# Twenty unread TensorE turns at the start of a one-core hybrid decoder layer, taken out

## The chip, the cores and the metric

One core of one Trainium2 chip runs the whole layer in one launch. The metric is the device time of that launch in microseconds (us); lower is better. The kernel before was timed three times: 916.11, 916.15 and 916.73 us, median 916.15 us.

## What is computed

The input is a residual stream `x` of 512 tokens by 1024 features and a conditioning row `c` of 1024 values. Cut to what matters here, the reference does:

```
mod = silu(c) @ w_ada + b_ada                       # 1024 x 6144 weights
sh1, sc1, gt1, sh2, sc2, gt2 = split(mod, 6)
h = rms_norm(x, g_norm_mix) * (1 + sc1) + sh1       # 512 x 1024
proj = h @ w_in                                     # columns split into branches
...                                                 # recurrence, attention, merge, x += ...
h2 = rms_norm(x, g_norm_ffn) * (1 + sc2) + sh2
x = x + (1 + gt2) * ((gelu(conv(u_gate)) * u_val) @ w_down)
return rms_norm(x, g_final)
```

The change lies in the first 20 us, where `h` is made: `x` has to be loaded, normalised by token and turned (TensorE works on features by tokens), and the first two parts of `mod` (`sh1` and `sc1`) have to be summed from `w_ada` before the turned `x` can be scaled.

## The kernel before, in words

The kernel has a hand-written instruction stream for each engine: TensorE (PE), VectorE (DVE), ScalarE (ACT), GpSimd (POOL), and SyncE (SP), which issues almost all DMAs. They meet at semaphores. PSUM's eight banks are handed out by a plan made ahead (`plan_banks`); `claim(engine, name)` waits until the bank planned for that name is free, `filled` and `ready` mark and await its contents.

Products are made in three passes over fp32r halves: high weights by high activations, low weights by high activations, high weights by low activations (`three_passes`, `grown`, L1311 is the matmul helper). Work is cut into units of 256 weight columns. Each unit's weights are loaded by SP, rounded to a high part by ACT (`w_hi`) and subtracted to a low part by POOL (`w_lo`, L813, or L824 at the start).

The first three units are "grown": they don't wait for all of `h`. The 1024 features are cut in four shares `j` of 256; as soon as share `j` of `h` exists, TensorE adds its part to the units (`growing_products(j)`).

The order at the start, engine by engine:

- SP loads `c`, the four token tiles of `x`, then for each share `j` the `w_ada` quarters (`ada_quarters(j)`, L628) and the three weight shares (`first_shares(j)`, L637). From `j = 2` on `ada_quarters` waits for the summed pair `j - 2` (`pair_done`), and at `j = 2` also for the bank `("mod1", 0)` to be filled by TensorE.
- ACT squares and sums the four tiles of `x` (L974), POOL takes the inverse root (L760, L761), ACT and DVE write the normalised `x`, two tiles each (`xn_in`, L977 and L1876).
- DVE sums `csilu * w_ada` feature tile by feature tile (`pair_sums`, L1833 to L1837) and, once TensorE has summed over the partitions, finishes `a1` and `mod` (`modulated`, L1849 to L1853).
- ACT then writes `h_hi` and `h_tmp` from the turned `x` (`first_h`, L944); POOL or DVE makes `h_lo` (L794, L1859).
- TensorE turns `c` (`"cT"`), waits for seven small vectors loaded by ACT's queue (`vec_in`) and turns them (`vector_rows`); then come the twenty unread turns, each a transpose of the identity by the identity into the bank claimed for `("xT", 0, 2)`, which nobody reads and which the real transpose overwrites. Then follow in program order: `transposed_x(0)` to `(3)` (16 transposes of `xn_in`, behind a wait for all four normalised tiles), `direct_sums` (16 matmuls of one column each, on `w_ada` itself), `transposed_x(4)`, `first_modulation(0)` (8 matmuls of one column), `transposed_x(5)` to `(7)`, and the four `growing_products`. All transposes go by the helper at L1314.

After that TensorE runs the other units of the input projection with the small products of recurrence and attention between them, the merge, the output projection, the up-projection in a loop, and the down-projection. Behind its last matmul ACT, DVE and POOL finish the norm, and SP stores.

Of the kernel before, what the change touches and what calls it, by code (L numbers as in the profile page):

```python
# [29 lines left out]
P = 128  # L30
# [196 lines left out]
def layer_kernel(nc, x, c, w_ada, b_ada, g_norm_mix, w_in, lb_logits, g_hg_norm, w_branch_a, w_branch_b, w_out,  # L227
                 g_norm_ffn, w_up, conv_w, conv_b, w_down, g_final, out):
    with ExitStack() as ctx:
# [97 lines left out]

        places = ((120, 136, 512), (128, 152, 512), (126, 150, 2048), (144, 160, 512), (168, 174, 512), (108, 114, 512))
        sl_raw = [three(f"sl_raw{i}", a, n) for i, (a, _, n) in enumerate(places)]
        sl_hi = [three(f"sl_hi{i}", b, n, F32R) for i, (_, b, n) in enumerate(places)]  # L330
        sl_lo = [three(f"sl_lo{i}", a, n, F32R) for i, (a, _, n) in enumerate(places)]
        kept = at("kept", 180, [P, 2, 512])
        corner = at("corner", 184, [P, 2, 512])
# [13 lines left out]
        def small(name, cols, rows=P, dt=F32):  # L347
            nonlocal off
            t = at(name, off, [rows, cols], dt)
            off += -(-cols * 4 // 32) * 32 / KB  # L350
            return t

        ident = small("ident", P)
# [108 lines left out]
        def claim(eng, name):  # L462

            b, n = BANKS[name]
            if n:
                eng.wait_ge(free[b], n)
            return bank[b]
# [841 lines left out]
        def _(pe):  # L1309
# [3 lines left out]
            def transpose(o, i):  # L1313
                return pe.transpose(o, i, ident[0:i.shape[0], 0:i.shape[0]])  # L1314
# [4 lines left out]
            b = claim(pe, "cT")  # L1319
            filled(transpose(b[:, 0:KT], c_rows[:, :]), "cT")  # L1320

            def vector_rows():

                pe.wait_ge(vec_in, 16 * 7)
                b = claim(pe, "vec")
                transpose(b[:, 0:N_VEC], vec_rows[:, :])
                filled(transpose(b[:, N_VEC:N_VEC + 88], conv_rows[:, :]), "vec")
# [316 lines left out]
                share_low(pe, j, 2)  # L1644
                grown(j, 2, wlo, h_hi, last=True)

            def unread_turns(name, n):

                b = claim(pe, name)
                for i in range(n):  # L1650
                    transpose(b[:, 0:P], ident[:, :])

            vector_rows()
            unread_turns(("xT", 0, 2), 20)
            for k in range(4):
                transposed_x(k)
            direct_sums()
# [855 lines left out]
```

## Time and profile before

| | us |
|---|---|
| median of three runs | 916.15 |
| lowest, highest | 916.11, 916.73 |
| the profiled execution, its own time | 915.85 |
| its span, first to last instruction | 914.1 |
| TensorE busy in it | 894.5 (98%) |
| mean granted TensorE clock, as a share of full speed | 0.997 |

The profile is one execution. Its span is 1.75 us shorter than the execution's own time, and that time is 0.30 us under the median. PE is the matmul row of TensorE, PEld its weight loads, which overlap with the matmuls; every transpose and every matmul has one load and one matmul. Ends of matmuls are modelled, so in a run of many the spacing of starts (its length divided by its count) says more of speed than the mean duration. "Idle before" an instruction names what ended that idle time.

### The profile page before, as it was taken

The numbers are of one execution on the slowest core, as the hardware profiler recorded it, in microseconds if no ns is written. First come the engines' busy times: TensorE is split into PE (matmuls) and PEld (weight loads), VectorE is DVE, ScalarE is ACT, GpSimd is POOL, SyncE is SP. The second block draws the span as 40 slices with busy tenths as digits, with TensorE's granted clock in tenths as the row PEclk, the third lists the DMA queues.
The fourth block names the chain that finished last, engine by engine and source line by source line (L and its number), as shares of the span: only waits on it lengthen the run. The fifth ranks groups of instructions, "written<-read, shape, count | busy, mean of one in ns | idle before, by whom it ended". The sixth has DMA issues, their size and how long they took to land.

```text
span 914.1 us, 11898 instructions
## 1 busy us (share of the span) xinstructions
PE 894.5 (98%) x4414; PEld 756.1 (83%) x4414; DVE 584.8 (64%) x839; ACT 392.1 (43%) x518; POOL 439.9 (48%) x373
## 2 busy tenths in 40 slices
PE   5999999999999999999999999999999999999996
PEld 5788898988888888888888888888888888888884
DVE  4845778675558978975634426555444455576997
ACT  5534434351534324353322326545544445433534
POOL 2679643454333442454544545866555656541005
PEclk9999999999999999999999999999999999999998
DMA  9922322112443868244535242334434433445552
GB/s 318 330 93 92 105 80 81 59 47 92 132 145 105 263 198 263 92 141 163 192 122 191 61 137 79 112 119 138 138 138 138 136 128 103 138 148 190 202 177 99
DMA packets 99512, 129.94 MB, mean 142 GB/s; under 512 B 3022, under 2 KB 85130, under 8 KB 99470
## 3 DMA queue, kind: packets, MB, share of 16 engines
q1 hardware_dynamic: 99240, 129.29, 42.7%
q8 instruction: 28, 0.46, 0.2%
q14 instruction: 14, 0.11, 0.0%
q10 hardware_dynamic: 230, 0.08, 0.0%
HBM read 127.23 MB, written 2.13 MB: 142 GB/s over the span
## 4 chain that ended last, share of the span: by engine, by line
PE 41%; issue 29%; POOL 23%; DVE 3%; DMA 1%; ACT 1%; POOLq 0%; ACTq 0%; DVEq 0%
PE bank L1311 40%; POOL w_lo L813 20%; PE bank L1314 1%; DVE sl_lo L2380 1%; POOL xg L879 1%; DMA conv_rows<-in_conv_b_dram 1%; POOL masks L749 1%; POOL masks L786 1%; DVE sl_raw L2373 0%; DMA sl_raw<-in_w_down_dram 0%; DVE xn_ffn L2250 0%; ACT h_hi L944 0%; ACTq L925 0%; POOL masks L784 0%; DVE mix_lo L2388 0%
## 5 line engine op out<-in xcount | busy, mean ns | idle before, releaser
L813 POOL TENSOR_TENSOR w_lo<-w_raw,w_hi 128x512 fp32r<-128x512 f32 x244 | 353.0, 1478 | 342.2 <-ACT w_hi L908 337.5
L1311 PE MATMUL bank<-h_hi,w_hi 128*128 128x512 f32 (+1 forms) x880 | 336.4, 389 | 1.0 <-issue 0.5
L1311 PE MATMUL bank<-h_lo,w_hi 128*128 128x512 f32 (+1 forms) x880 | 333.0, 386 | 0.0
L1311 PE MATMUL bank<-h_hi,w_lo 128*128 128x512 f32 (+1 forms) x880 | 260.2, 385 | 0.0
L1311 PEld LDWEIGHTS bank<-h_hi,w_hi 128*128 128x128 f32 x880 | 165.0, 188 | 35.2 <-issue 1.5
L1311 PEld LDWEIGHTS bank<-h_hi,w_lo 128*128 128x128 f32 x880 | 165.2, 188 | 33.2
L1311 PEld LDWEIGHTS bank<-h_lo,w_hi 128*128 128x128 f32 x880 | 165.3, 188 | 32.4
L908 ACT ACTIVATE w_hi<-w_raw 128x2048 fp32r<-128x2048 f32 x60 | 114.8, 1913 | 171.5 <-PE bank L1311 171.4
L1311 PE MATMUL bank<-sl_hi,mix_hi 128*128 128x512 f32 x110 | 42.8, 389 | 0.0
L1311 PE MATMUL bank<-sl_lo,mix_hi 128*128 128x512 f32 x110 | 42.8, 389 | 0.0
L1311 PE MATMUL bank<-sl_hi,mix_lo 128*128 128x512 f32 x110 | 42.8, 389 | 0.0
L2321 DVE TENSOR_TENSOR dn_raw<-dn_raw 128x1024 f32<-128x1024 f32 x11 | 17.0, 1546 | 37.7 <-DMA dn_raw<-in_w_down_dram 37.7
L1242 ACT ACTIVATE sl_hi<-sl_raw 128x1536 fp32r<-128x1536 f32 (+1 forms) x22 | 28.0, 1274 | 30.0 <-DVE sl_raw L2371 15.1
L1206 ACT ACTIVATE gated_up<-bank,convc 128x512 f32<-128x512 f32 x22 | 15.9, 775 | 57.3 <-PE bank L1311 57.3
L2310 DVE SCALAR_TENSOR_TENSOR gated_up<-bank,convc,gated_up 128x511 f32<-128x511 f32 x22 | 16.4, 745 | 37.0 <-ACT gated_up L1206 37.0
L879 POOL TENSOR_TENSOR xg<-x,gf_row 128x512 f32<-128x512 f32 x6 | 7.7, 1293 | 67.1 <-DVE sl_lo L2380 67.0
L2329 DVE TENSOR_TENSOR gated_up<-gated_up,bank 128x512 f32<-128x512 f32 x22 | 15.1, 688 | 38.2 <-PE bank L1311 38.2
L862 POOL TENSOR_TENSOR dn_lo<-dn_raw,dn_hi 128x512 fp32r<-128x512 f32 x22 | 27.9, 1291 | 19.5 <-ACT dn_hi L1220 19.4
L2380 DVE TENSOR_TENSOR sl_lo<-sl_raw,sl_hi 128x1536 fp32r<-128x1536 f32 (+1 forms) x22 | 32.6, 1484 | 1.4 <-ACT sl_hi L1242 1.4
L1813 DVE SCALAR_TENSOR_TENSOR part<-ada,csilu,part 128x256 f32<-128x256 f32 x48 | 30.0, 625 | 0.0
L1076 ACT ACTIVATE prob<-prob,nmax 128x128 f32<-128x128 f32 (+1 forms) x48 | 20.0, 417 | 22.6 <-DVE nmax L2104 22.4
L1311 PE MATMUL bank<-w_hi,m_hi 128*128 128x512 f32 x64 | 25.1, 392 | 0.2 <-POOL w_lo L813 0.2
(297 smaller groups left out, 1397.0 us busy)
## 6 DMA issues: line engine op xcount, KB each, us to landing
w_raw<-in_w_in_dram SPq DMA_DIRECT2D x31, 1024.0 KB, 5.2
w_raw<-in_w_up_dram SPq DMA_DIRECT2D x22, 1024.0 KB, 5.1
ada<-in_w_ada_dram SPq DMA_DIRECT2D x16, 1024.0 KB, 5.3
dn_raw<-in_w_down_dram SPq DMA_DIRECT2D x11, 1024.0 KB, 4.9
sl_raw<-in_w_down_dram SPq DMA_DIRECT2D x22, 512.0 KB, 3.4
ada<-in_w_ada_dram SPq DMA_DIRECT2D x32, 256.0 KB, 7.3
w_raw<-in_w_out_dram SPq DMA_DIRECT2D x4, 1024.0 KB, 5.0
w_raw<-in_w_in_dram SPq DMA_DIRECT2D x12, 256.0 KB, 7.2
```

The source lines that it names most:

```text
L813: ins = pool.tensor_tensor(wlo[slot][:, cols], raw[slot][:, cols], whi[slot][:, cols].bitcast(F32), ALU.subtract)
L862: ins = pool.tensor_tensor(dn_lo[:, b, :], dn_raw[:, 512 * (b + 1):512 * (b + 2)], dn_hi[:, b, :].bitcast(F32), ALU.subtract)
L879: pool.tensor_tensor(xg[:, t, cols], x1[:, t, cols], gf_row[:, cols], ALU.mult).then_inc(xg_done, 1)
L908: act.activation(whi[slot][:, :], raw[slot][:, :], ACT.Copy).then_inc(hi_done, 1)
L1076: ins = act.activation(prob[:, hh, at_:at_ + n], prob[:, hh, at_:at_ + n], ACT.Exp, scale=SCALE, bias=nmax[:, col:col + 1], accum_out=ssum ...
L1206: act.activation(gated_up[:, t, :], bank[bk][:, :], ACT.Identity, scale=CW[:, bass.ds(2 * i + (2 * FT + t), 1)], bias=CW[:, bass.ds(2 * i ...
L1242: act.activation(sl_hi[s_][:, 0:q, :], sl_raw[s_][:, 0:q, :], ACT.Copy).then_inc(slhi_done, 1)
L1311: return pe.matmul(o, lhsT, rhs, start=start, stop=stop, **kw)
L1813: ins = stt(dst, unit[:, k, :], sc, dst, ALU.mult, ALU.add)
L2310: stt(tt_, bank[bk][:, 0:S - 1], CW[:, bass.ds(2 * i + (FT + t), 1)], tt_, ALU.mult, ALU.add).then_inc(tap_done, 1)
L2321: tt(blocks[:, 1:3, :], blocks[:, 1:3, :], blocks[:, ::-3, :], ALU.subtract).then_inc(dn_diff, 1)
L2380: tt(sl_lo[s_][:, 0:q, :], sl_raw[s_][:, 0:q, :], sl_hi[s_][:, 0:q, :].bitcast(F32), ALU.subtract).then_inc(sllo_done, 1)
```

## The change

The helper and its one call are removed. Nothing is put in their place; no other engine's stream is edited.

```diff
-            def unread_turns(name, n):
-
-                b = claim(pe, name)
-                for i in range(n):
-                    transpose(b[:, 0:P], ident[:, :])
-
             vector_rows()
-            unread_turns(("xT", 0, 2), 20)
             for k in range(4):
                 transposed_x(k)
             direct_sums()
```

## Rows read from the trace of the kernel before

**Rows 1.** The page: TensorE's share, and its clock in 40 slices.

```profile
PE 894.5 (98%) x4414; PEld 756.1 (83%) x4414; DVE 584.8 (64%) x839; ACT 392.1 (43%) x518; POOL 439.9 (48%) x373
...
PEclk9999999999999999999999999999999999999998
```

**Rows 2.** Waits of TensorE over the span: total us, times, longest.

```profile
PE bank L1314 <- DMA conv_rows<-in_conv_b_dram: 7.0, 1, 7.0
PE bank L1314 <- DMA c_rows<-in_c_dram: 2.3, 1, 2.3
PE bank L1314 <- DVE xn_ffn L2250: 0.6, 1, 0.6
PE bank L1311 <- issue: 0.5, 1, 0.5
PE bank L1311 <- ACT h_hi L944: 0.5, 1, 0.5
PE bank L1311 <- POOL w_lo L813: 0.2, 1, 0.2
```

**Rows 3.** Timeline, TensorE's weight loads: start us, length us, what, count.

```profile
9.77 4.22 PEld L1314 LDWEIGHTS bank<-ident 128*128 128x128 f32 x20
14.19 1.88 PEld L1314 LDWEIGHTS bank<-ident,xn_in 128*128 128x128 f32 x16 [0.20 <-ACT xn_in L977]
16.04 1.87 PEld L1311 LDWEIGHTS bank<-csilu,ada 128*128 128x128 f32 x16
17.75 0.50 PEld L1314 LDWEIGHTS bank<-ident,xn_in 128*128 128x128 f32 x4
18.22 0.97 PEld L1311 LDWEIGHTS bank<-ones,part 128*128 128x128 f32 x8
19.03 1.38 PEld L1314 LDWEIGHTS bank<-ident,xn_in 128*128 128x128 f32 x12
```

**Rows 4.** Timeline, TensorE's matmuls in the same stretch.

```profile
9.59 0.39 PE L1314 MATMUL bank<-ident,vec_rows 76*128 76x76 f32 x1 [7.00 <-DMA conv_rows<-in_conv_b_dram]
9.77 0.35 PE L1314 MATMUL bank<-ident,conv_rows 88*128 88x88 f32 x1
9.92 4.47 PE L1314 MATMUL bank<-ident 128*128 128x128 f32 x20
```

**Rows 5.** Line L1314 and tile xn_in: ns min/median/max, first and last start.

```profile
L1314 PE MATMUL bank<-ident x20: 421/421/421, 9.9 to 14.0; 128*128 128x128 f32 x20
L1314 PE MATMUL bank<-ident,xn_in x32: 272/273/477, 14.2 to 20.4; 128*128 128x128 f32 x32
```

**Rows 6.** Windows: us, PE busy (instructions), granted clock, DMA share, GB/s.

```profile
14.40:14.60 0.20, 0.20 (x2) 1.00 1.10 343
14.60:14.80 0.20, 0.20 (x4) 1.00 1.06 338
...
905.50:906.00 0.50, 0.10 (x1) 1.00 0.00 0
906.00:908.00 2.00, 0.00 (x0) 1.00 0.65 262
908.00:908.50 0.50, 0.00 (x0) 1.00 0.00 0
908.50:909.00 0.50, 0.00 (x0) 0.85 0.00 0
```

**Rows 7.** Timeline of the start, the engines that TensorE meets.

```profile
11.95 2.19 ACT L977 ACTIVATE xn_in<-x_in,rstd 128x1024 f32<-128x1024 f32 x2 [1.44 <-POOL rstd L761]
19.31 0.17 DVE L1849 COPY part<-bank 128x4 f32<-128x4 f32 x1 [2.01 <-PE bank L1311]
20.23 1.45 ACT L944 ACTIVATE h_hi<-bank,mod,a 128x512 fp32r<-128x512 f32 x2 [1.11 <-DVE mod L1853]
21.11 1.36 PE L1311 MATMUL bank<-h_hi,w_hi 128*128 128x512 f32 x4 [0.46 <-issue]
```

**Rows 8.** SP's issue of the third `w_ada` share; DMA issues, KB each, us to landing.

```profile
19.54 5.91 SPq L628 DMA_DIRECT2D ada<-in_w_ada_dram  x8
...
ada<-in_w_ada_dram SPq DMA_DIRECT2D x32, 256.0 KB, 7.3
```

## The prediction

> **What bounds the kernel now.** I read the page's shares first, then TensorE's waits, then the timeline of the first 21 us, and last the windows around the two places where the clock could move. The share of busy time [rows 1] says that TensorE is the bound: 98% of the span. The waits [rows 2] say where the other 2% lies: 2.3 and 7.0 us ahead of the first two turns of small vectors, and then, over the remaining 900 us, four waits that sum to 1.8 us. The rest is the tail behind the last matmul, which ends at 905.6 us (0.10 us of work in the slice from 905.5 [rows 6]), 8.5 us ahead of the span's end. So from 9.59 us on TensorE is a belt without gaps: what makes its early work later moves everything behind it, and at most those 1.8 us could take any of it up.
>
> The twenty turns lie from 9.77 to 13.99 us in the row of loads [rows 3] and from 9.92 to 14.39 us in the row of matmuls [rows 4]. The next real work, the first transpose of the normalised x, has its load at 14.19 us, 0.20 us after the last load of a turn, and what ended that idle time is ACT's write of `xn_in`: 11.95 + 2.19 = 14.14 us [rows 7]. So the turns fill a wait that ends elsewhere. They hold nobody up.
>
> What the reader is to see next is speed. Twenty turns took 4.22 us, 211 ns each; the last twelve transposes of x, instructions of the same form and size, took 1.38 us, 115 ns each [rows 3]. A turn's duration is 421 ns, the same for all twenty, and the median of the transposes is 273 ns, with 477 ns at the worst [rows 5]. The slice up to 14.60 us touches two matmuls, the next one four [rows 6]. So TensorE ran at its lower level (1.2 GHz) from 9.6 to about 14.55 us and at its upper level (2.4 GHz) after that, though the clock column prints 1.00 all the way [rows 1, 6]; durations decide here, and I take it that the column has no record for the time before the rise. The rise came 4.96 us after the work at 9.59 us began, with 22 turns of one kind or another and nothing else between. At the other end the column does show a fall: it is 0.85 in the slice from 908.5 to 909.0, so the level halved at 908.5 + 0.35 = 908.85 us, 3.2 us after the last matmul's end.
>
> **The change, part by part.** *The turns' own time.* 20 x 211 ns go out of a wait that x ends. Removed cost on the path: 0. Bounds: the last turn ends at 14.39 us, 0.20 us behind the first load of x, so the gain is between 0 and 0.2 us. I take 0, since the load went ahead at once.
>
> *The clock at 14.19 us.* In the changed kernel TensorE does two small turns at 9.6 us and then nothing for some 4 us. I expect it to meet x at the lower level, and to rise only after working on. The wait for the rise is the unknown. The nearest row is the rise of this very trace, 4.96 us after work began: from 14.19 us that gives 19.15 us. The low end is the only other change of level in the trace, the fall 3.2 us after the last work: 17.4 us. The lowest thinkable end is that the level is high at once: no loss. For the high end see the second rival.
>
> *What the lower level costs until 19.15 us.* Each slow us does 115/211 = 0.545 us of full-speed work, so 4.96 us of it lose 0.455 x 4.96 = 2.26 us. Counted by instructions: 16 transposes x 211 ns end at 14.19 + 3.38 = 17.57 us; the direct sums run at 1.71/16 = 107 ns at the upper level (starts 16.04 to 17.75 [rows 3]) and, if a load is their limit like a turn's, at 211 ns at the lower; 7.5 of them fit ahead of 19.15 us, the other 8.5 take 0.91 us, end 20.06 us against 17.75 us now: 2.31 us. I take 2.3 us. With the low end (3.2 us) it is 0.455 x 3.2 = 1.5 us.
>
> *Is that stretch on the path?* DVE sat idle 2.01 us until TensorE's sum for share 0 was there at 19.3 us, ACT idle 1.11 us for DVE, and TensorE itself idle 0.46 us ahead of its first product at 21.11 us [rows 7]. The chain runs from the transposes through `direct_sums` and `first_modulation(0)` to `modulated(0)`, `h_hi` and the first product, and all behind it is the belt. The loss passes whole. It also moves the second share, since its sums on DVE begin only behind `modulated(0)` and the copies of the turned x.
>
> *The queues that wait for it.* SP issues the third `w_ada` share at 19.54 us, right behind TensorE's fill of ("mod1", 0) [rows 8]. That goes 2.3 us later. A load of 256 KB lands 7.3 us after issue while the queue is this full [rows 8], so what was issued before covers the gap, and since its readers move by the same 2.3 us I take 0. The cover ends when the delay nears some 5 us. POOL's and ACT's parts of the weight shares only gain slack. No other engine's stream changes: 0.
>
> Sum: 0 + 2.3 + 0 = 2.3 us. The profiled execution's own time, 915.85 us, becomes 918.15 us; on the median, 0.30 us higher, it is 918.45 us, and I say **918.4 us**, +0.25%. A difference of 0.2%, 1.8 us, is about what a measurement of this kernel can tell from none.
>
> **The rivals.** *The turns raise nothing (ends at no change).* The rise at 14.55 us would then belong to something that stays: a fixed moment of the execution, or x's own transposes. Place: the first transposes at 14.19 us. Price: nothing, or the 0.2 us of the last turn's end as a gain, so 915.95 to 916.15 us. It decides if the rise still comes at about 14.6 us with nothing ahead of it but two small turns. For it: the rise fell 0.36 us behind the first load of x, which may be no accident, and the clock column never showed a low level there. Against it: eight microseconds of DMA waits before went by without a rise, and 4.96 us of unbroken work is what stands ahead of it. The Trainium skill, in TensorE: Matmul & The Clock Gate, section PE-mode transpose, has a rule by which it would come out so: transposes don't count as work for the gate, so the turns could not have raised it and their removal would be free, 916.15 us. The trace speaks against that rule, since nothing but transposes had run when the level rose. Chance 12%.
>
> *The rise comes later than 4.96 us after x.* In the kernel before the engine had only dense 128-column turns ahead of the rise. In the changed one 16 of them are followed by the direct sums, 4 more and the 8 sums of `first_modulation(0)`, and the level may not have risen by their end. At the lower level all 44 instructions up to the end of `first_modulation(0)` take 44 x 211 ns = 9.3 us against 5.1 us now (14.19 to 19.28): +4.2 us, 920.4 us; if the first products must run slow too, each slow us costs half of itself and another 4.96 us cost 2.3 to 2.5 us more, with 0.5 us for the twelve transposes, up to 923.3 us. Near 5 us of delay the loads, too, would begin to run dry. For it: no row shows a rise during these sums of one column. Against it: the level didn't fall during the same 24 instructions between 16.0 and 19.3 us, so they held it at least. Chance 15%, between 919.4 and 923.3 us.
>
> *The loss is taken up behind.* The four waits behind 21 us [rows 2] are all the slack there is, 1.8 us; three of them follow TensorE's own work through another engine and so move with it, and only the wait for `w_lo` (0.2 us) and a part of the others could close. At best 2.3 - 1.2 = 1.1 us stay, 917.2 us. Chance 5%.
>
> **How the numbers follow.** My forecast, 917.6 to 919.4 us by its two bounds and the play of the moment of the rise, has 66%. The two named cases of no or little change have 12% and 5%, the late rise 15%, and 2% are left for a gain that I can't name. The range 916.9 to 921.0 us holds the forecast, the taken-up loss and most of the late rise (some 11 of its 15): 8 in 10. Slower by over 0.2% (beyond 918.0 us): the late rise and the forecast but for its lowest part (10%, a rise 3.2 to 4.0 us after x), 56 + 15 = 71%. Within 0.2%: 12 + 5 + 10 = 27%. Faster: 2%.
>
> **What would show each step.** Right: TensorE idle from about 10.1 to 14.19 us; the sixteen transposes of x 211 ns apart, their durations 421 ns and not 273; a speed-up between 17.4 and 21 us; the first product of `h_hi` near 23.4 us instead of 21.11; the same shift at the last matmul (907.9 for 905.6 us); DMA share at 1.1 through the start with no hole near 22 us. Wrong: x's transposes 115 ns apart from the start (first rival); one-column matmuls and the first products still slow beyond 21 us (second); a shift at 23 us that is gone by the last matmul (third). The whole step falls if x's first transpose moves away from 14.19 us.

## The result and the profile after

The changed kernel takes 920.44 us, the median of nine executions (918.56 to 921.38), against 916.73 us for the kernel before, timed beside it (nine executions, 915.89 to 918.01). The ratio is 1.0038, 95% interval 1.0030 to 1.0046: slower, by 3.7 us, clear of the 0.2% that can be told apart. The nine lie in two groups, four between 918.56 and 919.38 us and five between 920.44 and 921.38 us. The profiled execution belongs to the upper one: its own time is 921.38 us, 5.5 us above that of the profiled execution of before, its span 919.7 us, 5.6 us above.

First the page and the waits of TensorE (columns as in [rows 1] and [rows 2]).

```profile
PE 896.1 (97%) x4394; PEld 757.7 (82%) x4394; DVE 584.0 (64%) x839; ACT 391.8 (43%) x518; POOL 442.1 (48%) x373
...
PEclk9999999999999999999999999999999999999998
```

```profile
PE bank L1314 <- DMA conv_rows<-in_conv_b_dram: 7.0, 1, 7.0
PE bank L1314 <- ACT xn_in L977: 4.3, 1, 4.3
PE bank L1314 <- DMA c_rows<-in_c_dram: 2.3, 1, 2.3
PE bank L1314 <- DVE xn_ffn L2243: 0.6, 1, 0.6
PE bank L1311 <- ACT h_hi L944: 0.5, 1, 0.5
PE bank L1311 <- POOL w_lo L813: 0.2, 1, 0.2
```

One wait is new, 4.3 us for `xn_in`: the gap that the turns filled. None of the others grew, and the one put down to "issue" ahead of the first product (0.5 us) is gone. TensorE's busy time even rose, from 894.5 to 896.1 us, though twenty turns are gone: what remains took longer. Where, the timeline of its weight loads shows, beside [rows 3].

```profile
14.47 3.27 PEld L1314 LDWEIGHTS bank<-ident,xn_in 128*128 128x128 f32 x16 [4.60 <-ACT xn_in L977]
17.73 3.53 PEld L1311 LDWEIGHTS bank<-csilu,ada 128*128 128x128 f32 x16
21.00 0.90 PEld L1314 LDWEIGHTS bank<-ident,xn_in 128*128 128x128 f32 x4
21.89 1.83 PEld L1311 LDWEIGHTS bank<-ones,part 128*128 128x128 f32 x8
23.45 2.61 PEld L1314 LDWEIGHTS bank<-ident,xn_in 128*128 128x128 f32 x12
26.05 1.27 PEld L1311 LDWEIGHTS bank<-h_hi,w_hi 128*128 128x128 f32 x4
27.36 0.89 PEld L1311 LDWEIGHTS bank<-h_hi,w_lo 128*128 128x128 f32 x4
```

The shift against before grows step by step: 0.28 us at the first transpose of x (which itself came later here), 1.69 at the direct sums, 3.25 at the next transposes, 3.67 at the sums of `first_modulation(0)`, 4.42 at the last twelve transposes, 4.97 at the first product, 5.28 at the fifth (matmuls at 22.30 before and 27.58 us after). The last twelve transposes end 5.65 us later (their loads at 20.41 us before, 26.06 us after); the 0.67 us without a load that the kernel before has ahead of its first product take that back to 4.97. After that it stands: the first product of the second share starts 5.29 us later (31.13 before, 36.42 after). The matmul rows of after, with the last one:

```profile
26.12 1.63 PE L1311 MATMUL bank<-h_hi,w_hi 128*128 128x512 f32 x4
27.58 1.09 PE L1311 MATMUL bank<-h_hi,w_lo 128*128 128x512 f32 x4
...
910.77 0.39 PE L1311 MATMUL bank<-sl_hi,mix_lo 128*128 128x512 f32 x1
```

The fifth product and the last matmul of before:

```profile
22.30 1.09 PE L1311 MATMUL bank<-h_hi,w_lo 128*128 128x512 f32 x4
...
905.21 0.39 PE L1311 MATMUL bank<-sl_hi,mix_lo 128*128 128x512 f32 x1
```

The last matmul starts at 910.77 us, 5.56 us later than the 905.21 us of the kernel before; the spans differ by as much. So 5.3 of the 5.6 us were lost ahead of 27.6 us and passed through to the end, and nothing was taken up.

The speed is in the tile's own line (ns min/median/max, first and last start), beside [rows 5]:

```profile
L1314 PE MATMUL bank<-ident,xn_in x32: 417/421/472, 14.5 to 26.0; 128*128 128x128 f32 x32
```

All 32 transposes of x are slow, not sixteen: median 421 ns, where it was 273 ns. The clock column prints 1.00 here too, so the rise is read from spacings. The four first products take 1.46 us (26.12 to 27.58), 365 ns each on the mean; the following ones take 225 to 233 ns each, and where four such products all ran slow (the run with split sums and no turns, below, matmuls from 26.44 to 28.29 us) they took 463 ns each. So two or three of the four ran slow: TensorE stayed at 1.2 GHz until about 27.1 us and ran at 2.4 GHz from there. That is the case of the prediction's second rival, the late rise, and not of the forecast.

The other engines behave as priced. VectorE waits for the first sum, then ScalarE for VectorE; SyncE issues the third `w_ada` share 4.35 us later than in [rows 8]:

```profile
23.84 0.16 DVE L1842 COPY part<-bank 128x4 f32<-128x4 f32 x1 [6.22 <-PE bank L1311]
23.89 3.95 SPq L628 DMA_DIRECT2D ada<-in_w_ada_dram  x8
24.76 1.45 ACT L944 ACTIVATE h_hi<-bank,mod,a 128x512 fp32r<-128x512 f32 x2 [1.82 <-DVE mod L1846]
```

Behind that the DMA share sinks: it is 1.06 between 24 and 26 us, 0.87 between 28 and 30 and 0.80 between 34 and 36, where the kernel before holds 1.10 or 1.11 up to 42 us. That is the hole that the prediction put at some 5 us of delay. TensorE's list of waits shows none for a load there, and the shift stays at 5.3 us meanwhile, so it cost nothing.

### The profile page after: what moved, and what is told of

Its sections match the earlier page's. It is cut to its first block, busy times and chain, and to the rows that moved or that the text cites. A ratio compares the mean times of both kernels' runs of the same rounds, so it can differ in the third digit from the quotient of the medians.

```text
span 919.7 us, 11858 instructions
## 1 busy us (share of the span) xinstructions
PE 896.1 (97%) x4394; PEld 757.7 (82%) x4394; DVE 584.0 (64%) x839; ACT 391.8 (43%) x518; POOL 442.1 (48%) x373
## 4 chain that ended last, share of the span: by engine, by line
PE 41%; issue 29%; POOL 24%; DVE 3%; DMA 1%; ACT 1%; POOLq 0%; SPq 0%; DVEq 0%; ACTq 0%
PE bank L1311 40%; POOL w_lo L813 20%; PE bank L1314 1%; DVE sl_lo L2373 1%; DMA x_in<-in_x_dram 1%; POOL xg L879 1%; POOL masks L786 1%; POOL masks L749 1%; DMA sl_raw<-in_w_down_dram 0%; DVE sl_raw L2366 0%; DVE xn_ffn L2243 0%; ACT h_hi L944 0%; ACT xn_in L977 0%; DVE mix_lo L2381 0%; DVE h_tmp2a L1897 0%
```

## The experiments

Two theories were put against each other. The clock: TensorE meets x at the lower level, and the loss is the time until the level rises. The rival: the 20 instructions' place in the code, or work of any kind between 9.8 and 14.2 us, or x and the loads coming later. The runs were made in three groups, and the kernel before was timed beside each; its medians were 916.49, 916.61 and 916.74 us.

**The changed kernel again** (no edit).

> The changed kernel, unedited, profiled and timed once more. Theory (the clock): TensorE meets x at the lower level, the sixteen transposes of x lie some 205 to 211 ns apart, and the rise comes anywhere between the end of those transposes (17.5 us) and the first products (27 us); a rise at 27 us gives about 921 us, one at 20 us about 918.7 us, so that the spread of the executions (918.6 to 921.4 us) is the spread of the rise. Rival (something else, such as x or a weight share landing later, or the placing of the instructions): the time does not follow the moment of the rise.

Median 920.54 us over six executions (917.80 to 922.58). The profiled one took 919.40 us, of the lower group, and its clock column, unlike the other's, has a record in this stretch (columns as in [rows 6]):

```profile
20.00:22.00 2.00, 2.00 (x20) 1.00 1.11 348
22.00:23.00 1.00, 1.00 (x10) 0.86 1.10 348
23.00:26.00 3.00, 2.98 (x9) 0.50 1.10 348
26.00:27.00 1.00, 1.00 (x5) 0.94 1.11 349
```

```profile
14.89 3.28 PEld L1314 LDWEIGHTS bank<-ident,xn_in 128*128 128x128 f32 x16 [5.13 <-ACT xn_in L977]
18.15 2.42 PEld L1311 LDWEIGHTS bank<-csilu,ada 128*128 128x128 f32 x16
20.41 0.51 PEld L1314 LDWEIGHTS bank<-ident,xn_in 128*128 128x128 f32 x4
```

Sixteen slow transposes; then the direct sums speed up within their row (2.26 us for sixteen, against 3.27 all slow and 1.71 all fast), so the level rose at about 19.3 us. It fell again at 22.7 us (0.86 is 0.72 us at full and 0.28 us at half speed) and rose for good at 26.1 us. TensorE was busy all that time: the fall came among the last twelve transposes of x, 0.8 us behind the last of 24 one-column pairs (20.99 + 0.95 = 21.94 us), and not in idle time. So this execution has the forecast's rise, some 4.4 us after x, and then pays again. Its first product starts 2.66 us later than before, of which 0.70 us are x's own later arrival and 1.96 us the 4.4 slow us; the ninth starts 3.55 us later (26.78 against 23.23), so the second low stretch cost 0.9 us.

The mean granted clock of each execution shows how many are of which pattern. A level that is low from the start leaves no record in the column, a second low stretch does. Of the fifteen executions of the changed kernel the seven between 917.80 and 919.40 us have 0.995 or 0.996, the eight between 920.44 and 922.58 us have 0.997 or 0.998, without exception. So the lower group is the pattern with a rise soon after x and a recorded low stretch behind it, the upper group that of the first profile.

**One column instead of 128.** In the first form twenty one-column matmuls stood in the turns' place.

```diff
-                    transpose(b[:, 0:P], ident[:, :])
+                    mm(b[:, 0:1], ident[:, :], ident[:, 0:1])
```

> The kernel before, with its twenty turns made one column wide (identity by the first column of the identity): the same number of instructions at the same place, still unread, each with a whole weight load. Theory (the clock rises on wide work, not on loads with one column): no rise before x, TensorE meets x at the lower level, 918.5 to 921.5 us like the changed kernel. Rival (placing of the instructions, or any work at all between 9.8 and 14.2 us raises the level): a rise near 14.5 us and 916 to 917 us like the kernel before.

Median 924.25 us (922.10 to 926.57, four executions). The size was a miss of mine: the trace has 40 pairs of load and matmul, two for each of the twenty matmuls in full precision, where a transpose has one. They took 8.6 us and pushed x to 18.0 us, and so the time above the expected range. Halved, the run is the clean one:

> The kernel before with its twenty turns replaced by ten unread one-column matmuls (twenty loads and twenty matmuls in the trace, each matmul of full precision being done in two): the same 4.2 us of work at the same place without the columns. Theory (wide work raises the level, one-column work does not): the twenty pairs end near 14.0 us, x is met at the lower level, no rise until at least 17 us, time 918.5 to 922.5 us as the changed kernel. Rival (any 4.2 us of work, or the placing of the instructions): rise near 14.5 us, time 916 to 917 us.

Median 921.38 us (918.51 to 922.83, five executions), ratio 1.0044 (1.0026 to 1.0063), the changed kernel's time. Its loads and first products:

```profile
10.21 4.39 PEld L1311 LDWEIGHTS bank<-ident 128*128 128x128 f32 x20
14.62 3.27 PEld L1314 LDWEIGHTS bank<-ident,xn_in 128*128 128x128 f32 x16
17.88 3.54 PEld L1311 LDWEIGHTS bank<-csilu,ada 128*128 128x128 f32 x16
...
26.20 1.19 PEld L1311 LDWEIGHTS bank<-h_hi,w_hi 128*128 128x128 f32 x4
```

The same number of loads, in the same place, for 4.4 us in place of 4.2 and right up to x, and the sixteen transposes of x are as slow as with no turns at all; the level rises near 27 us. Neither the placing of twenty instructions nor being busy was what the turns gave. What was taken from them is their 128 columns, and with them their being transposes: a plain matmul of 128 columns in the turns' place was not run, so the two are not told apart.

**Turns ahead of the small vectors.** Thirty turns in the earlier wait, none behind it.

```diff
+            unread_turns(("xT", 0, 2), 30)
             vector_rows()
-            unread_turns(("xT", 0, 2), 20)
```

> The kernel before with thirty unread turns put ahead of the small vectors' turns (from 2.5 us on, in the wait for them), and none behind. Theory: the level rises at about 7 us (2.5 + 5), the turns end near 8 us, TensorE then idles from 10 to 14.2 us but for the two small turns; the level falls about 3.2 us after the last work, near 13.2 us, and x is met at the lower level again: 918.5 to 921.5 us, and the clock column shows the fall. If it doesn't fall in that gap, x is met at the upper level and the time is 915.7 to 916.3 us. Rival (turns raise nothing): no early rise in the trace, time as the changed kernel's.

Median 920.97 us (918.25 to 923.77, seven executions). The turns took 4.66 us for thirty: three or four loads in each half us up to 5.6 us and six from there, so the level rose at about 5.6 us. Then the column shows the fall and the long low stretch:

```profile
12.00:12.50 0.50, 0.00 (x0) 0.90 1.10 352
12.50:14.00 1.50, 0.00 (x0) 0.50 1.10 348
14.00:19.00 5.00, 4.47 (x22) 0.50 1.10 348
...
27.50:29.00 1.50, 1.50 (x5) 0.50 0.87 287
29.00:30.00 1.00, 1.00 (x5) 0.77 0.98 330
```

The level fell at 12.4 us, 5.1 us behind the last turn's load (2.66 + 4.66 = 7.32 us) and some 2.4 us behind the two small turns at 9.6 us. It was at half from there on, through 15 us of a busy TensorE, and rose at 29.5 us. Here the column itself says what had to be inferred elsewhere. (At 923.01 us this execution is among the slow ones of the seven; the three below 920 us have a mean clock of 0.992 in place of 0.988 to 0.990, so their low stretch was shorter.) A level gained early is worth nothing if it isn't held to x.

**Ten turns in place of twenty.**

> The kernel before with ten turns in place of twenty (they end near 12 us, 2.2 us idle ahead of x). Theory: half the work ahead of x raises the level only in some executions, so the times are a mixture of 916 to 917 and 918.5 to 922 us, median between the two kernels, 917 to 920 us. Rival (only the first work counts, however short): 916.5 us as the kernel before. Rival (placing): no relation with the rise in the trace.

Four executions: 918.17, 921.45, 922.67 and 922.78 us, median 922.06, ratio 1.0064 (1.0049 to 1.0080). No execution near 916 us was among them, and the median lies above the expected 917 to 920 us, so ten turns with 2 us of idle time behind were worth no more than none. Whether they were too few or ended too early this run does not separate. The profiled one, the fastest, met x at the lower level (sixteen transposes in 3.4 us) and rose at about 17.6 us, as the direct sums began. It fell again at 21.0 us, 0.3 us behind the one-column sums:

```profile
20.00:22.00 2.00, 2.00 (x15) 0.75 1.10 348
22.00:23.00 1.00, 1.00 (x7) 0.50 1.11 350
23.00:26.00 3.00, 3.00 (x12) 0.77 1.10 347
```

**Wide work behind x.** Sixteen turns between the transposes of x and the direct sums of the changed kernel.

```diff
+            unread_turns(("mod1", 0), 16)
             direct_sums()
```

> The changed kernel with sixteen unread turns between the sixteen transposes of x and the direct sums, so that wide work goes on for up to 6.8 us from x on. Theory (the one-column sums are what puts the rise off): the rise comes by 17.5 to 21 us in every execution, never near 27 us; the turns themselves cost 1.8 to 3.4 us on the path, so the time is 919.5 to 922 us, with less spread than the changed kernel's 3 to 5 us. Rival (the moment of the rise has nothing to do with what kind of work there is): rises up to 27 us as in the changed kernel, and a time of 922 to 925 us.

```profile
15.25 3.23 PEld L1314 LDWEIGHTS bank<-ident,xn_in 128*128 128x128 f32 x16 [5.12 <-ACT xn_in L977]
18.45 1.78 PEld L1314 LDWEIGHTS bank<-ident 128*128 128x128 f32 x16
20.20 1.87 PEld L1311 LDWEIGHTS bank<-csilu,ada 128*128 128x128 f32 x16
```

Median 920.03 us (919.05 to 921.52, four executions). In the profile the rise came at about 18.4 us, 3.1 us behind the first load of x: the sixteen turns take 111 ns each and everything behind them is fast. That rise came as x's own sixteen transposes ended, ahead of the first turn, so in this execution the turns did not bring it about; the changed kernel does the same sixteen and rises there in some executions and not in others. What speaks for the turns is that all four executions lie below 921.6 us: a late rise as in the changed kernel's upper group (920.44 to 922.58 us) with at least 1.8 us of turns on top would be 922.2 us or more (an estimate from these runs). Work that nobody reads, put on the path for 1.8 us, costs no time against the changed kernel's 920.5 us.

**One-column sums split up.** The direct sums in two halves with the fourth set of transposes between, first with no turns:

```diff
-            for k in range(4):
+            for k in range(3):
                 transposed_x(k)
-            direct_sums()
+            direct_sums((0, 1))
+            transposed_x(3)
+            direct_sums((2, 3))
```

> The changed kernel (no turns) with the direct sums split in two and the fourth set of transposes of x between the halves. Theory (the level stays low as long as it does because sixteen one-column matmuls in a row follow x's transposes): wide work is spread over the stretch, the rise comes by about 21 us instead of up to 27 us, 918 to 920 us, below the changed kernel's 920.4 us. Rival (wide work has to be unbroken to raise the level): the mixture never raises it ahead of the first products, rise at 26 to 27 us in every execution, 921 to 922.5 us, with less spread.

The rival of that expectation holds in the times: 921.72 to 922.48 us in four executions, median 922.04. In its loads wide and narrow work alternate, and all of it is slow:

```profile
14.90 2.42 PEld L1314 LDWEIGHTS bank<-ident,xn_in 128*128 128x128 f32 x12 [5.50 <-ACT xn_in L977]
17.30 1.83 PEld L1311 LDWEIGHTS bank<-csilu,ada 128*128 128x128 f32 x8
18.87 0.90 PEld L1314 LDWEIGHTS bank<-ident,xn_in 128*128 128x128 f32 x4
...
26.37 1.40 PEld L1311 LDWEIGHTS bank<-h_hi,w_hi 128*128 128x128 f32 x4
27.87 1.58 PEld L1311 LDWEIGHTS bank<-h_hi,w_lo 128*128 128x128 f32 x4
```

The rise came at about 29.4 us, later than the 26 to 27 us of the rival and the latest but one of all. All four have a mean clock of 0.997 or 0.998, that of the late rise. So the runs that meet x at the lower level can be put in order by what follows x before the first one-column sum: behind twelve transposes none of four executions rose early, behind sixteen 15 of 35 (seven of fifteen in the changed kernel, two of four and two of five with one-column matmuls, three of seven with early turns, one of four with ten turns, all by their times and mean clocks), behind sixteen transposes and sixteen turns four of four. That fits the reading that, from the lower level, an unbroken stretch of wide work raises it and one-column sums put the rise off. With so few executions, and profiles of one each, it is argued and not shown.

**Two attempts at a better kernel.** Turns both ahead of and behind the small vectors:

```diff
+            unread_turns(("xT", 0, 2), 30)
             vector_rows()
-            unread_turns(("xT", 0, 2), 20)
+            unread_turns(("xT", 0, 2), 28)
```

> The kernel before with thirty unread turns ahead of the small vectors' turns and twenty-eight behind, in place of twenty behind. Theory: the rise comes near 7 us and the level is kept to x in every execution; the later 28 turns are 115 ns each and end by 13.3 us, ahead of x at 14.2 us. The executions lose their spread: 915.8 to 916.2 us each, median 0.3 to 1 us below the kernel before. Rival (the rise belongs to a fixed moment or to x): same as the kernel before, with its spread up to 918 us. If the level is still low at 9.8 us, the 28 turns end at 15.7 us and delay x by 1.5 us: 917.6 us.

The level did rise at about 7 us, x was met at the upper level, and two idle stretches of 1.8 and 2.0 us ahead of it did not lose it:

```profile
14.99 1.73 PEld L1314 LDWEIGHTS bank<-ident,xn_in 128*128 128x128 f32 x16 [2.01 <-ACT xn_in L977]
```

```profile
20.00:21.00 1.00, 1.00 (x10) 0.86 1.11 349
21.00:24.00 3.00, 2.96 (x9) 0.50 1.10 349
24.00:25.00 1.00, 1.00 (x6) 0.94 1.11 348
```

But then it fell, at 20.7 us, with TensorE busy, after the same one-column sums, and five of the first eight products ran slow. The spread got wider, not narrower: eleven executions lie between 915.55 and 922.32 us, and a twelfth took 1527.31 us at a mean granted clock of 0.557, which nothing here explains. The median of the eleven, 916.48 us, is that of the kernel before (916.49); of all twelve it is 916.97 us. The ratio, of the eleven, is 1.0016 (0.9999 to 1.0032). The four slowest of them, 919.11 to 922.32 us, have the lowest mean clocks, 0.991 to 0.994. So a rise before x does not secure what comes after it.

Twenty turns with the split sums:

> The kernel before, twenty turns kept, with the direct sums split in two and the fourth set of transposes of x between the halves, so that no long stretch holds one-column work alone. Theory (the executions of the kernel before above 917 us are those in which the level falls behind the one-column sums near 21 us): fewer falls, median 916.0 us, 0.3 to 0.7 us below the kernel before, highest below 918 us. Rival (the spread comes from x landing at 14.2 to 15 us): nothing gained, 916.3 to 916.7 us. If the second half of the sums or the wait for the fourth quarter of the weights now delays x's transposes, ScalarE's copies are later but hidden: 0.

> The kernel with twenty turns and the split direct sums once more, to settle whether it beats the kernel before: 916.0 to 916.4 us with no execution above 917.5 us, 0.2 to 0.5 us below the kernel before, which is within what can be told apart; if its median lies at or above the kernel before, there is no gain.

Medians 916.25 us against 916.61 and 916.65 us against 916.74 (ratios 0.9996, 0.9987 to 1.0005, and 0.9999, 0.9990 to 1.0008). All 22 executions lie between 915.81 and 917.36 us, those of the kernel before timed beside them (31) between 915.37 and 919.21. The spread may be narrower; a gain is not shown. Nor did the split do away with the falls: the three slowest executions of the second run (916.98 to 917.36 us) have mean clocks of 0.995 or 0.996, as the kernel before has in the six of its 22 executions above 917 us that were timed beside the first group.

The second of these profiles also settles two rivals. x's first load lies at 14.83 us in it, later than the 14.47 us of the changed kernel's profile, and its transposes are fast from the first one:

```profile
14.83 1.30 PEld L1314 LDWEIGHTS bank<-ident,xn_in 128*128 128x128 f32 x12 [0.43 <-ACT xn_in L977]
```

The execution took 916.50 us, so a later x is not what costs 3.7 us. And its twenty turns took 4.21 us, as slow as in the kernel before, up to 14.41 us: the level rose between them and x, so x's own transposes did not bring it about.

## Why the prediction was right or wrong

The direction, the mechanism and the range held: slower, by TensorE's clock at the start, 920.44 us inside 916.9 to 921.0. The value, 918.4 us, was 2.0 us too low: 0.6 of that is the kernel before, 916.73 us here against the 916.15 us that I had started from, and the rest the change itself, 3.7 us against 2.3. The case that decided the median was the one that I had given 15%.

*The turns' own time: 0.* Right. The wait that they filled appears as idle time, 4.3 us. The first transpose of x did come 0.28 us later, but x's arrival moves from profile to profile (14.19 to 15.25 us, leaving out the run with twenty one-column matmuls), so no price can be given to that.

*The clock at 14.19 us: low.* Right in both profiles of the changed kernel, and in every other one without at least twenty turns directly ahead of x.

*The wait for the rise: 4.96 us.* This is the step that failed. I carried the one rise of the trace of before over to a stretch with different work in it. In the profile it was 12.6 us (14.47 to about 27.1), in the repetition 4.4 us with a second low stretch of 3.4 us behind it, for which the sum had no term. The reading that "the level didn't fall during the same 24 instructions between 16.0 and 19.3 us" was a fact of one execution and no rule: in four profiles it fell right behind them.

*What a slow us costs.* Right. The prediction had 9.3 us for the 44 pairs up to the end of `first_modulation(0)`; the trace has 9.37 us, from 14.47 to VectorE's start at 23.84 us. The forecast's own price holds too: 0.455 us for each slow us, and 1.96 us for 4.4 in the repetition (0.45). The last twelve transposes, slow too, put off the first product by a further 0.5 us, as that case had it, and the slow first products cost 0.3 us more. The second rival's own number without slow products, 920.4 us, is the median; that is luck in part, since the median is the lowest of the upper group and the kernel before was 0.6 us slower here.

*It passes whole.* Right: 5.3 us at 27.6 us are 5.6 us at the last matmul. The case that it is taken up behind, 5%, has nothing for it (and the 1.2 us that it took off stand in no row).

*The queues: 0 up to some 5 us.* Right: SyncE's issue moved by 4.35 us, the DMA share dipped, nobody on the path waited.

*The turns raise nothing (12%).* Wrong, by the run with ten one-column matmuls: same place, nearly the same length, no width, and the loss is there in full; and by the level that had risen before x in the run with split sums. The rule of the Trainium skill that stood beside it (TensorE: Matmul & The Clock Gate, section PE-mode transpose: transposes don't count as work for the gate) is not borne out by these traces: with full-precision transposes alone ahead of it the level rose at about 5.6 and 7 us in the two profiles with thirty early turns, at 14.55 us with twenty (and at 14.7 us, ahead of x, in the second run with split sums), and at 18.4 us at the end of sixteen of x, while one-column matmuls in the turns' place raised nothing.

What stays open is why one execution of the changed kernel rises after 4 us and the next after 12. Each pattern has one profile of this kernel; the mean clocks say that they are the whole of it (four of nine, then three of six, with the early rise), and not what chooses between them. Nor is it shown why the level falls again behind the early rise.

## What to carry to other kernels

A filler that nobody reads is not dead code if it keeps TensorE's clock up ahead of a stretch on the path: look at the spacing of identical instructions (211 against 115 ns here) before calling it free to remove. Here twenty transposes of 128 columns did that work, one-column matmuls and ten transposes did not, and a level raised early was lost in a gap of 4.8 us and kept over two of some 2 us. A filler is free only if it lies wholly in a wait that something else ends. And when an event of the clock is carried over from a trace, compare what kind of work lies in the stretch, not only how long it is; one execution shows one of several patterns.

## What the hardware did that I had not expected

The level fell while TensorE had work all the time: at 22.7 us in the repetition, at 21.0 us with ten turns and at 20.7 us with turns on both sides, each time within some 1 us behind a stretch of one-column matmuls, and it was up again only at 26.1, 24.4 and 24.1 us. The run with twenty one-column matmuls has a fourth such fall, at 25.3 us, up again at 28.7. The fall at 12.4 us in the early-turns run lies in an idle gap of 4.8 us. The advice of the Trainium skill (TensorE: Matmul & The Clock Gate, section Why this matters for your kernels) is to leave no long idle gaps between bursts of matmuls. It covers that last fall, but not the other four. That the one-column sums caused them is argued from where they lie: the kernel before does the same sums and its profile has no fall there.

The clock column prints 1.00 until its first record, and that record is the rise: the trace's list of clock changes, counted from the start of the span, begins at 14.56 us in the kernel before, 27.12 us in the changed one, 19.30 us in its repetition, 27.09 us with ten one-column matmuls, 18.38 us with sixteen turns behind x and 29.38 us with split sums and no turns. The moments read from spacings above agree with it to 0.1 us. With the level low from the start, it prints full speed up to 27 us in the changed kernel's profile and up to 29 us with split sums and no turns; only the run whose level rose and fell early has 0.50 in those same slices.

A one-column matmul in full precision shows as two pairs of load and matmul, each taking about as long as a whole 128-column transpose at either level (4.39 us for twenty pairs, 219 ns each, against 211 at the lower; 107 against 115 at the upper). So the 16 and 8 one-column matmuls that this text counts in `direct_sums` and `first_modulation(0)` are eight and four in the kernel.
